# A router's product with its weights stationary in two column halves of the array, and a second small product that turns and sums the logits

## The reference

```python
h2 = rms_norm(x, norm_ffn_g)                       # (T, 1024), f32
lg = h2 @ w_rg                                     # 4 group logits
g_idx = argmax(lg)
le = (h2 @ w_re).reshape(T, 4, 8)[g_idx]           # 32 expert logits, those of the group
top_v, top_i = top_k(le, 2)
expert_id = g_idx * 8 + top_i
combine = softmax(lg)[g_idx] * softmax(top_v)
```

## Time and profile before

| | us |
|---|---|
| median of 3 runs | 2202.96 (2202.63 to 2206.08) |
| profiled execution, its own time | 2202.57 |
| its span | 2200.8, granted clock 0.977 |
| PE busy | 2088.1 |
| DVE busy | 1623.4 |
| ACT busy | 1260.0 |
| POOL busy | 806.9 |

### The profile page before, as it was taken

The page is one execution under the profiler, slowest core; times in us unless marked ns, Lnnn a source line. Parts: engine busy times, 40 slices in busy tenths (PEclk is TensorE's granted clock), DMA queues, the critical chain, the costliest instruction groups (busy, mean ns, idle before and its releaser), DMA issues. The chain is left out here.

```text
span 2200.8 us, 40164 instructions
## 1 busy us (share of the span) xinstructions
PE 2088.1 (95%) x13505; PEld 1771.5 (80%) x13506; DVE 1623.4 (74%) x2083; ACT 1260.0 (57%) x2200; POOL 806.9 (37%) x689
## 2 busy tenths in 40 slices
PE   8999999995899999899999895999999999999998
PEld 6888888884687887678787774888888888888887
DVE  3799999984777667867878967969698556556644
ACT  5322433335677777866676643768588555456533
POOL 1111544553566654545545435222222222222221
PEclk9999999996999999999999996999999999999999
DMA  7553344334333242333222117989899968767852
GB/s 228 186 191 134 118 128 159 120 106 144 114 117 109 80 131 81 108 105 116 80 73 92 54 70 258 361 281 372 308 357 373 329 197 282 228 198 264 285 172 35
DMA packets 211517, 393.17 MB, mean 179 GB/s; under 512 B 54749, under 2 KB 81757, under 8 KB 211389
## 3 DMA queue, kind: packets, MB, share of 16 engines
q1 hardware_dynamic: 197853, 357.42, 47.1%
q0 software_dynamic: 13536, 34.12, 6.8%
HBM read 315.42 MB, written 91.23 MB: 185 GB/s over the span
## 5 line engine op out<-in xcount | busy, mean ns | idle before, releaser
L2428 DVE TENSOR_TENSOR p_w_lo<-p_raw,p_w_hi 128x1024 fp32r<-128x1024 f32 (+1 forms) x260 | 439.5, 1728 | 150.5 <-ACT p_w_hi L2223 149.9
L2051 POOL TENSOR_TENSOR p_wgt<-p_wgt,p_past 128x1024 f32<-128x1024 f32 (+4 forms) x166 | 308.5, 1859 | 347.2 <-DVE p_past L1929 347.1
L2223 ACT ACTIVATE p_w_hi<-p_raw 128x2048 fp32r<-128x2048 f32 (+1 forms) x198 | 361.8, 1859 | 84.0 <-PE p_up L2310 67.3
L762 DVE SCALAR_TENSOR_TENSOR p_ut<-p_ut,p_cw 128x512 f32<-128x512 f32 (+1 forms) x480 | 329.2, 762 | 0.0
L1929 DVE TENSOR_TENSOR_SCAN p_past<-p_keep,p_past,p_one 128x513 f32<-128x513 f32 (+1 forms) x196 | 225.9, 1193 | 75.3 <-ACT p_keep L1746 73.3
L1746 ACT ACTIVATE p_keep<-p_zp 128x512 f32<-128x512 f32 (+3 forms) x326 | 158.8, 547 | 119.2 <-PE p_zp L1620 106.5
L2310 PE MATMUL p_gp<-p_w_hi,p_xt_hi 128*128 128x256 f32 x736 | 210.4, 286 | 0.0
L436 PE MATMUL p_pj<-p_w_hi,p_xt_hi 128*128 128x512 f32 x512 | 205.2, 401 | 4.2 <-DVE p_xt_lo L738 2.4
L2310 PE MATMUL p_gp<-p_w_lo,p_xt_hi 128*128 128x256 f32 x736 | 206.5, 281 | 0.0
L2310 PE MATMUL p_gp<-p_w_hi,p_xt_lo 128*128 128x256 f32 x736 | 206.4, 280 | 0.0
L436 PE MATMUL p_pj<-p_w_hi,p_xt_lo 128*128 128x512 f32 x512 | 200.6, 392 | 0.0
(11 more groups left out here) (309 smaller groups left out, 4975.6 us busy)
## 6 DMA issues: line engine op xcount, KB each, us to landing
p_raw<-in_w_up SPq DMA_DIRECT2D x128, 512.0 KB
p_raw<-in_w_gate SPq DMA_DIRECT2D x128, 512.0 KB
p_raw<-in_w_down SPq DMA_DIRECT2D x128, 512.0 KB
wide_raw<-in_w_in SPq DMA_DIRECT2D x56, 256.0 KB, 3.8
wide_raw<-in_x SPq DMA_DIRECT2D x17, 512.0 KB
scr_y<-wide_raw SPq DMA_DIRECT2D x17, 512.0 KB, 3.1
wide_raw<-scr_y SPq DMA_DIRECT2D x17, 512.0 KB
y_out<-wide_raw SPq DMA_DIRECT2D x17, 512.0 KB, 2.9
```

The lines of the kernel that those rows point to most:

```text
L762: dve.scalar_tensor_tensor(dst, src, cw[:, a, j:j + 1], dst, ALU.mult, ALU.add).then_inc(tap_done, 1)
L2051: pool.tensor_tensor(mine, mine, past_rows[:, u % NP, 0:n, 2:2 + w], ALU.mult).then_inc(a_done, 1)
L2223: act.activation(part(w_hi, p, wide), raw[:, n % RING:n % RING + wide, :], ACT.Copy).then_inc(whi_done, wide)
L2428: dve.tensor_tensor(part(w_lo, p, wide), raw[:, n % RING:n % RING + wide, :], part(w_hi, p, wide).bitcast(F32), ALU.subtract).then_inc(wlo ...
```

## The change

The router's weights are stationary now (128 x 36), the turned h2 moves (128 tokens). Even chunks write to partitions 0 to 35 of the bank, odd ones to partitions 64 to 99, the two column halves of the array. So the bank holds two partial sums of the logits, with the tokens along the free axis. ACT copies these 100 x 128 values to `zt`, which is the place of h2t's chunk 0. A new job, `logit`, at least a step later, multiplies zt (stationary) with `fold`, a 128 x 36 matrix with ones where row = column and row = column + 64: that turns the logits back and adds both sums. DVE then copies `lg` and `le` from the bank of `logit`.

Since zt lies in the first half of h2t, the second group (c = 1) is turned first, and the first only behind the logit of the tile before. Batches are picked behind their last logit. A step may have a third job if that is a logit.

```diff
-            return ("h2t", job[1] - 2, 1) in where
+            return ("h2t", job[1] - 2, 0) in where
         if job[0] == "h2t" and job[1] > NT:
-            return ("route", job[1] - 1) in where
+            return ("logit" if job[2] == 0 else "route", job[1] - 1) in where
...
-        for _ in range(3 if s < 10 or mid <= s < mid + 10 or s >= end - 1 else 2):
-            ok = sorted(x for x in waiting if x[2] <= s and allowed(x[3]))
+        wide = s < 10 or mid <= s < mid + 10 or s >= end - 1
+        for n in range(3):
+            ok = sorted(x for x in waiting if x[2] <= s and allowed(x[3]) and (wide or n < 2 or x[3][0] == "logit"))
...
-            elif job[0] == "h2t" and job[2] == 1:
+            elif job[0] == "h2t" and job[2] == 0:
                 later(("route", job[1]), s + 1, s + 3)
-            elif job[0] == "route" and job[1] - NT == BATCHES[BATCH_OF[job[1] - NT]][1] - 1:
+            elif job[0] == "route":
+                later(("logit", job[1]), s + 1, s + 3)
+            elif job[0] == "logit" and job[1] - NT == BATCHES[BATCH_OF[job[1] - NT]][1] - 1:
...
-            [("route", z)], [], [], [("rank", len(BATCHES) - 1)]]
+            [("route", z)], [("logit", z)], [], [], [("rank", len(BATCHES) - 1)]]
...
+        zt, fold = h2t[0:HD + NR, 0, :], sb("fold", [P, NR])
...
-        pick_step = {b: where["route", NT + hi - 1] for b, (lo, hi) in enumerate(BATCHES)}
+        pick_step = {b: where["logit", NT + hi - 1] for b, (lo, hi) in enumerate(BATCHES)}
...
+                elif j[0] == "logit":
+                    r = j[1] - NT
+                    pe.wait_ge(zt_done, r + 1)
+                    pe.wait_ge(fold_done, 3)
+                    last = pe.matmul(bank[:, 0:NR], zt, fold[0:HD + NR, :], start=True, stop=True)
...
                     for k in range(KT):
-                        last = pe.matmul(bank[:, 0:NR], h2t[:, k, :], wr[:, k, :], start=(k == 0), stop=(k == KT - 1))
+                        x = k % 2 * HD
+                        last = pe.matmul(bank[x:x + NR, 0:P], wr[:, k, :], h2t[:, k, :], start=(k < 2),
+                                         stop=(k >= KT - 2), skip_group_check=True)
...
                     r, c = j[1] - NT, j[2]
-                    if r and c == 0:
-                        act.wait_ge(mp_full, use["route", j[1] - 1] + 1)
+                    if r:
+                        act.wait_ge(mp_full, use["route" if c else "logit", j[1] - 1] + 1)
...
+                elif j[0] == "route":
+                    act.activation(zt, mp[0:HD + NR, use[j] % 2, 0:P], ACT.Copy).then_inc(zt_done, 1)
...
+                pool.memset(fold[:, :], 0.0).then_inc(fold_done, 1)
+                for x in range(2):
+                    pool.wait_ge(fold_done, x + 1)
+                    pool.affine_select(out=fold[:, :], in_=fold[:, :], compare_op=ALU.not_equal, fill=1.0, base=-x * HD,
+                                       pattern=[[-1, NR]], channel_multiplier=1).then_inc(fold_done, 1)
```

More of the change, by code:

```diff
@@ L1129, in allowed @@
             return ("wo", NT - 1, 1) in where
-        if job[0] == "route":
+        if job[0] == "logit":
             b = BATCH_OF[job[1] - NT]
@@ L1155, in attention_jobs @@
                 then = s + 5 if s < end or job[1] == 2 * NT - 1 else s + 2
[L1156 to L1158 removed]
+                later(("h2t", job[1], 1), then, then + 2)
+                later(("h2t", job[1], 0), then + (1 if then < end - 1 else 0), then + 2)
+            elif job[0] == "h2t" and job[2] == 0:
                 later(("route", job[1]), s + 1, s + 3)
[L1160 removed]
+            elif job[0] == "route":
+                later(("logit", job[1]), s + 1, s + 3)
+            elif job[0] == "logit" and job[1] - NT == BATCHES[BATCH_OF[job[1] - NT]][1] - 1:
                 later(("rank", BATCH_OF[job[1] - NT]), s + (6 if s < end - 6 else 4), s + 7)
@@ L1164, in attention_jobs @@
     z = 2 * NT - 1
-    tail = [[], [], [("wo", z - 1, 0)], [("h2t", z - 2, 0), ("h2t", z - 2, 1)], [("o", z)],
-            [("wo", z - 1, 1), ("mix", z), ("route", z - 2)], [("wo", z, 0), ("h2t", z - 1, 0), ("h2t", z - 1, 1)],
-            [("wo", z, 1)], [("route", z - 1)], [("h2t", z, 0), ("h2t", z, 1), ("rank", len(BATCHES) - 2)],
-            [("route", z)], [], [], [("rank", len(BATCHES) - 1)]]
+    tail = [[], [], [("wo", z - 1, 0)], [("h2t", z - 2, 1), ("h2t", z - 2, 0)], [("o", z)],
+            [("wo", z - 1, 1), ("mix", z), ("route", z - 2)],
+            [("logit", z - 2), ("wo", z, 0), ("h2t", z - 1, 1), ("h2t", z - 1, 0)], [("wo", z, 1)],
+            [("route", z - 1)], [("logit", z - 1), ("h2t", z, 1), ("h2t", z, 0), ("rank", len(BATCHES) - 2)],
+            [("route", z)], [("logit", z)], [], [], [("rank", len(BATCHES) - 1)]]
     assert sorted(j for x in tail for j in x) == sorted(j for s in placed if s >= end for j in placed[s])
@@ L1321, in phase_attend @@
             y_step[m] = max(y_step[m], end_step[m - 3] + (5 if m - 3 >= NT else 1))
-        act_cost = {"k": 8, "q": 7, "o": 8, "mix": 6, "h2t": 6}
-        dve_cost = {"k": 8, "q": 7, "mix": 7, "wo": 7, "route": 3, "rank": 20}
+        act_cost = {"k": 8, "q": 7, "o": 8, "mix": 6, "h2t": 6, "route": 3}
+        dve_cost = {"k": 8, "q": 7, "mix": 7, "wo": 7, "logit": 3, "rank": 20}
         by_act = []
@@ L1684, in job @@
             def job(j):
-                if j[0] not in ("k", "q", "o", "mix", "h2t"):
+                if j[0] not in ("k", "q", "o", "mix", "h2t", "route"):
                     return
@@ L1782, in squares @@
                     act.wait_ge(st_h[r % 2], 16 * (r // 2))
-                    act.wait_ge(mp_full, use["h2t", m - 2, 1] + 1)
+                    act.wait_ge(mp_full, use["h2t", m - 2, 0] + 1)
                 act.activation(h2[:, r % 2, :], y[:, m % 3, :], ACT.Square, accum_out=ss).then_inc(ss_done, 1)
@@ L1892, in job @@
                                       ALU.add).then_inc(y_done, 1)
-                elif j[0] == "route":
+                elif j[0] == "logit":
                     x = j[1] - NT - BATCHES[BATCH_OF[j[1] - NT]][0]
```

9 lines of the change are left out of this document (6 added, 3 removed).

## The result

The changed kernel takes 2218.65 us (median of 4 runs, 2215.55 to 2224.64) beside 2202.8 of the kernel before in the same session: ratio 1.0074, 95% interval 1.0053 to 1.0094. That is some 16 us slower, where no change was forecast (2202.6) and the range ended at 2208.0.

The account below looks back on a forecast made before the run. PE was taken to set the pace of the attention steps, though not alone, and a chain between engines the tail's end. Steps -5.1 and tail +4.7 gave -0.4 us: forecast 2202.6 us, range 2197.5 to 2208.0.

Parts of the forecast that it names:

- the new product's time: Router product on PE: 0.86 us a tile instead of 1.81, saving 0.95 before what comes with it.
- its weight loads overlap: Router product: loads overlap passes, 0.054 us a pass; the rival without overlap gave 2206.9 us, chance 0.05.
- the fold's price: Added small product with the stacked identities on PE: 2 passes, 0.23 us a tile.
- the tail: From route 31 to the MoE phase's start: links sum to 4.75, taken as +4.7 us, ends 3.5 and 6.
- link 3: Tail: both halves of picks 3 fall between the last y eviction and hidden(33), delaying it by 3.1 us more.
- PE's sum: Attention steps: 14 tiles at 0.72 us saved, less 1.6 for switches, take 8.5 us from PE.
- the sentence on the banks: Attention steps: each logit job takes one more two-bank turn, with waits for DVE as behind the old route; no size given.
- Six tenths arrive: Attention steps: of the 8.5 us saved on PE, six tenths shorten the time, -5.1 us.
- The upper end of the range: Attention steps: +3 us if none of PE's saving arrives and one new wait is added.
- Half clock was priced in the tail: Tail: last transposes at half clock after PE's idleness, link +1.05 us; route 33 also at half clock, link -0.35.
- The slower rival: DVE keeps the attention steps' pace, only the tail's +4.7 us remains: 2207.7, with one new wait 2210.7; chance 0.19.
- The rival without halves: Router product gets no gain from array halves: 3.2 + 5.1 + 1.3 = +9.6 us, 2212.6; chance 0.03.

Follow-up runs that it names:

- e2: Changed kernel with the third last tile's logit in step 171 instead of 172, so the last picks start a step earlier; 2214.56 us, ratio to before 1.0057.
- e4: Kernel before with the new product alone, jobs at old places, small product in other columns of the route's bank; 2200.45 us, ratio to before 0.9993.
- e16: e9 with the small product of the fourth batch's first tile one step later; 2196.88 us, ratio to before 0.9968.
- e11: Kernel before with four more 128 x 4 copies a tile on DVE; ratio to before 1.0000.
- e6: Changed kernel with first three ranks one step earlier, third last tile's logit in step 171, h2's first half turned first; 2206.48 us, ratio to before 1.0019.
- e9: e4 with the small product written, start=False, to spare columns of the output values' bank; 2197.91 us, ratio to before 0.9964.
- e10: Kernel before with eight more router passes a tile on PE; ratio to before 1.0056, +12.3 us.
- e1: Changed kernel with the first three rank jobs one step earlier; 2211.95 us, ratio to before 1.0052.
- e8: e4 with the small product written, start=True, to spare columns of the output values' bank; 2185.15 us, not comparable because fewer expert blocks ran.

## Why the prediction was wrong

**Right:** the new product's time and that its weight loads overlap; the copy on ACT (0.28 to 0.34 us, 0.28 taken); the fold's price; and the tail, 4.0 us longer where 4.75 was worked out, with link 3 as described: both halves of the picks ahead of hidden 33, 5.2 us behind the eviction, then half clock. e2 took exactly this link away: its tail is 3.0 us shorter in the trace, its time 4.1 by medians.

**PE's sum was of the right size, as far as can be told.** 8.5 us were to go from PE in the steps. Against the profiled execution of before, 5.4 (e4) to 6.8 us (e16) went from its busy time. Against e11, which has before's PE work at the granted clock of e4 and e16 (0.98) and 293.96 us busy, it was 7.9 to 9.3.

**The step that failed** is the sentence on the banks: "Each logit job takes one more turn of the two mp banks; whoever comes two jobs later waits for DVE's copies, as it did behind the old route". It put the wait of whoever comes two jobs later at what it was, that is at nothing new. What counts is whom the new order makes neighbours: 14 more jobs in a ring of two banks brought rank, logit and o into one step (5.86 and 3.18 us), h2t behind a rank (2.93), the logit third behind k and q (2.76, 2.29, 1.73), and h2t to a hidden that stands behind DVE's picks (5.46). The order of the jobs is fixed by the program, so these neighbours could be read off before any run; the prediction goes through none of them for who would wait for DVE. By medians the ranks' places are worth 6.7 us and the order of the halves 2.4, neither clear of noise alone (4.8 and 2.9 by ratios); with the tail's picks, 12.1 together, which is clear. What is left of the places is 5.7 (e6 to e4), and the bank held by the fold 6.4 by ratios (e4 to e9; 2.5 by the medians of two sessions). By ratios that is the way from after to e9: 24.2 us.

**"Six tenths arrive"** failed with it. I took the share of a saving that arrives from PE's and DVE's busy shares, 94% and 82%. They didn't tell it: added PE work arrives nearly whole (e10), and a saving of the same size arrived as 1.5 us (e4), as 7.9 (e9) or, with a tail 4 us longer, as a loss of 16, by the jobs' places and by which bank the fold writes. The upper end of the range, +3 with one new wait, had one wait where the trace has 14.0 us of them net.

**Half clock was priced in the tail and forgotten in the steps.** PE's busy time in the steps is 293.95 us in after, 290.98 in e2 with the same order there, and 284.65 in e16 with the same products at other places. An estimate from these: passes at 1.2 GHz behind the new waits cost 6.3 (e2) to 9.3 us (after). Idle time 14.0 us longer and 9.3 of slower work, less 6.8 of saved work, are the 16.5 us of after's profiled steps, its slowest execution; with e2's, nearer to the median, it is 13.9 + 6.3 - 6.8 = 13.4.

**The slower rival had the sign and not the mechanism.** If DVE kept the steps' pace, e10's work on PE would have gone into its idle time, and e1 and e6, with DVE's work unchanged, could not have been shorter. Its figure with one new wait, 2210.7, was closer than the forecast for a reason that the runs don't bear out; that is luck. The rival without halves adds a term of 1.3 us for which the prediction gives no source; no run shows it, and the halves were used.

**Open:** how much of e9's gain over e4 is real (2.5 to 6.4 us), why e16's shorter steps in the trace don't show in its timed runs, and how much DVE work the changed kernel would hide. No run here has an order of jobs that gives the whole saving.

## What to carry to other kernels

Where engines share a ring of buffers in one fixed order, a new job is priced by its neighbours: list for each job who stands two places ahead, what the evicting engine has to do before it comes to that, and compare the lists before and after. Busy shares don't tell whether a saving arrives; adding the same amount of work at the same place tells whose pace it is, but not that taking it away pays; and what was added is to be measured in its own rows, since instructions overlap. A change of an instruction's form is best first tried with every job left at its old place.

## What the runs showed of the hardware

Waits of a few us cost PE more than their length. Behind the wait of 5.46 us (timeline of after, PE: h2t, transposes, values, scores) rows are at the 1.2 GHz level for 5.5 us:

```profile
1270.43 1.09 PE L1576 MATMUL p_mp<-p_ident,p_h 128*128 128x128 f32 x4 [5.46 <-DVE p_h L1971]
1271.32 1.91 PE L1645 MATMUL p_tp<-p_ident,p_wgt 128*128 128x128 f32 x8
1273.16 1.97 PE L1673 MATMUL p_op<-p_at,p_v 128*64 128x128 f32 x16
...
1275.97 0.40 PE L1634 MATMUL p_zp<-p_kt,p_q_hi 128*128 128x512 f32 x1
```

and even behind one of 2.29 us the clock falls a little later, though PE had been at work without a pause in between:

```profile
1230.58 0.41 PE L1582 MATMUL p_mp<-p_fold,p_h2t 100*128 100x36 f32 x2 [2.29 <-DVE p_kt L1891]
1230.92 1.50 PE L1673 MATMUL p_op<-p_at,p_v 128*64 128x128 f32 x16
1232.35 0.80 PE L1634 MATMUL p_zp<-p_kt,p_q_hi 128*128 128x512 f32 x1
1232.94 0.63 PE L1635 MATMUL p_zp<-p_kt,p_q_lo 128*128 128x512 f32 x1
```

A score product takes 0.63 us there for 0.40 at full clock. The first output of e8, with a start in 36 columns of the bank of the values, is off by half its size, and that of e9, without a start there, is not. That agrees with the Trainium skill, page "PSUM — Partial Sum Buffer", section "The four PSUM rules": a first product clears the written marks of the whole bank in the quadrants that it writes, not of its own columns alone.

Copies of 128 x 4 on DVE, each 0.15 us long in the trace, follow each other at 0.07 us: four of them cost 0.27 us.
